# All rows of the second expert table summed by TensorE, with VectorE's share of them removed

## The chip, the cores and the metric

The kernel runs on one core of one Trainium2 chip. The metric is the device time of one execution in microseconds (us), shown as the median of the runs. Engines: PE = TensorE, DVE = VectorE, ACT = ScalarE, POOL = GpSimd, SP = SyncE.

## What is computed

Two transformer blocks on 512 tokens of 1024 features, all in f32. The first has two kinds of attention, cross attention to a memory and a feed-forward part; the second has window attention, gated linear attention and, last, a feed-forward part of looked-up experts (PEER). Only this last part is touched by the change:

```python
q = (h @ wq).reshape(B, S, 8, 2, 128)
sub_scores = einsum('bshpk,hpnk->bshpn', q, subkeys)        # two times 128 keys a head
top_v, top_i = lax.top_k(sub_scores, 16)
cand = top_v[..., 0, :, None] + top_v[..., 1, None, :]      # 16 x 16 sums
best_v, best_pos = lax.top_k(cand, 16)
expert = ...                                                # 16 experts for each of 8 heads: 128 a token
gates = softmax(best_v)
# by blocks of 128 tokens:
ub = take(u, eb)                                            # 128 rows of 1024 for each token
hid = gelu(einsum('tkd,td->tk', ub, xb)) * gb
vb = take(v, eb)
y = einsum('tk,tkd->td', hid, vb)
```

The result is scaled by a row of gates, added to the residual, and normalised.

## The kernel before

The 512 tokens are four blocks of 128, with tokens on the partitions. Everything up to about 1472 us (projections, attentions, feed-forward) is left as it is by the change. The rest is the expert part, one block after another.

**Gather.** POOL (the issue is line 474) fetches, for each block, first the 128 rows of table u and then the 128 rows of table v. One "row" is an indirect DMA that brings each of the 128 tokens its own row of 1024 f32, 512 KB in all. The rows go in turn into a ring of eight slots (RING = 8), so a table is 16 turns (TURNS). Before each issue POOL waits until slot k is free (semaphore slot_free[k]); ahead of each turn it copies eight indices (line 466). The landing raises row_landed[k].

**Up stage.** For each of the 128 rows of u, DVE takes the dot product of row and token (`hidden`, line 1494) and frees the slot. Eight results at a time are copied into `hid`. Then ACT applies gelu (line 737) and DVE multiplies by the gates (`weights`, line 1513), which gives the 128 weights of each token.

**Down stage.** The rows of v are summed with these weights, by two engines that share the slots. SHARED is the list of PE's slots, 1, 3, 5 and 7. For each of these ACT makes a diagonal of 128 weights in `wdiag` (lines 766 to 769; it waits until the slot's row of the turn before has been used) and PE multiplies it with both halves of the row (`add_rows`, line 1095), which adds up in PSUM banks 0 and 1. The rows in slots 0, 2, 4 and 6 are DVE's (`weighted`, line 1523): acc = row * weight + acc, in SBUF. PE takes its rows in order of the slots, DVE its own likewise, and each frees the slot it has used.

**Picking.** `pick(b, q, step)` chooses the experts of one quarter of a block (two heads) in four steps, all on DVE. For block b + 1 its 16 steps are spread over block b's down stage: after each turn of `weighted` comes one step. For block 0 they stand in its up stage. Two additions of the mixer's output for blocks 2 and 3 (`add_mixed`) come after turns 4 and 8 of block 0's down stage.

**End of a block.** `add_experts` (lines 1526 to 1534) waits for slots 7 and 6, adds the two banks to acc (1531), multiplies by the gate row (1533) and adds to the residual X (1534). Behind it on DVE stand the next block's dot products. `prepare` (line 1508) clears acc during each up stage. On PE the late transposes and query projections of blocks 2 and 3 follow block 0's rows and wait for its residual.

```python
for i, k in enumerate(SHARED):
    pe.wait_ge(wdiag_ready, n * len(SHARED) + (len(SHARED) * TURNS * b + i + 1))
    pe.wait_ge(row_landed[k], n * 16 + 16 * (base + 1))
    for half in range(2):
        ins = pe.matmul(bank[half][:], wdiag[:, i, :], ring[k][:, half * COLS:(half + 1) * COLS], ...)
    ins.then_inc(slot_free[k], 1)
```

Of the kernel before, what the change touches and what calls it, by code (L numbers as in the profile page):

```python
# [23 lines left out]
ALU = mybir.AluOpType  # L24
# [41 lines left out]
RING = 8  # L66
TURNS = SLOTS // RING
QUARTERS = 4
CHUNKS = 2 * QUARTERS
SHARED = range(1, RING, 2)  # L70

# [17 lines left out]
def late(*event):  # L91

    return G_OUT2 + LATE.index(event)
# [27 lines left out]
def build(nc, A, out):  # L121
    ctx = ExitStack()
    with ctx:
        def sb(name, shape, dt=F32):
            return ctx.enter_context(nc.sbuf_tensor(name, shape, dt))

        def sem(name):
            return ctx.enter_context(nc.semaphore(name))

        bank = [ctx.enter_context(nc.psum_tensor(f"bank{i}", [P, COLS], F32)) for i in range(8)]  # L130
# [13 lines left out]
        GATE = sb("gate_rows", [P, 2, D])  # L144
# [81 lines left out]
        def scr(lo, n, dt=None, **dims):  # L226
            v = SCR[:, lo:lo + n]
            v = v.bitcast(dt) if dt else v
            return v.rearrange("p (a b) -> p a b", **dims) if dims else v
# [5 lines left out]
        hid, wgt = scr(1184, 128), scr(1312, 128)  # L235
# [4 lines left out]
        ring = [W[:, 2 - 2 * (k // 4), D * (k % 4):D * (k % 4 + 1)] for k in range(RING)]  # L240
        onehot = [t[:, 0:TOPK * CAND].rearrange("p (k c) -> p k c", c=CAND)
                  for t in (levelmask[:].rearrange("p a b -> p (a b)"), SCR[:, 2048:3072])]
        acc = SCR[:, 3072:4096]
        wdiag = GROW[:, 0:P * len(SHARED)].rearrange("p (a b) -> p a b", b=P)

# [7 lines left out]
        row_landed = [sem(f"row_landed{i}") for i in range(RING)]  # L253
# [19 lines left out]
        slot_free = [sem(f"slot_free{i}") for i in range(RING)]  # L273
        hid_copied, hid_ready, hid_gelu, wgt_ready = map(sem, ("hid_copied", "hid_ready", "hid_gelu", "wgt_ready"))
        wdiag_ready = sem("wdiag_ready")
        fin_x, fin_rms, fin_ready = map(sem, ("fin_x", "fin_rms", "fin_ready"))
# [209 lines left out]
        def _(act):  # L486
# [273 lines left out]
            for b in range(NB):  # L760
# [4 lines left out]
                with act.Fori(0, TURNS) as it:  # L765
                    for i, k in enumerate(SHARED):
                        act.wait_ge(slot_free[k], it + (base + 1))
# [14 lines left out]
        def _(pe):  # L782
# [303 lines left out]
            def add_rows(b):  # L1086
# [3 lines left out]
                def turn(n, first, last):  # L1090
# [4 lines that stand above are left out]
                            ins = pe.matmul(bank[half][:], wdiag[:, i, :], ring[k][:, half * COLS:(half + 1) * COLS],  # L1095
                                            start=(first and i == 0), stop=(last and i == len(SHARED) - 1))
                        ins.then_inc(slot_free[k], 1)
# [53 lines left out]
        def _(dve):  # L1151
            steps = [0]

            def link(ins):
                steps[0] += 1
                ins.then_inc(dve_step, 1)
                dve.wait_ge(dve_step, steps[0])
# [102 lines left out]
            for r in range(48):  # L1260
                dve.wait_ge(ada_landed[r % 3], 16 * (r // 3 + 1))
                dve.tensor_tensor_reduce(out=ada[:, r % 3, :], in0=ada[:, r % 3, :], in1=crow, scale=1.0, scalar=0.0,
                                         op0=ALU.mult, op1=ALU.add, accum_out=mod[:, r:r + 1]).then_inc(ada_used, 1)
# [5 lines left out]
            for i, (scale, gc) in enumerate(((8, GC_ATT2), (32, GC_PEER))):  # L1269
                dve.scalar_tensor_tensor(out=scol[:, i, :], in0=mod[:, scale:scale + KT], scalar=1.0, in1=gcol[:, gc, :],  # L1270
                                         op0=ALU.add, op1=ALU.mult)
# [21 lines left out]
            for b in range(NB):  # L1293
                for half in range(2):
                    i = STATS[N_Y] + 2 * b + half
# [3 lines left out]
                    ins = dve.tensor_scalar(y, y, rstd[:, i:i + 1], None, ALU.mult)  # L1299
                ins.then_inc(xn_ready, 1)  # L1300
            for b in range(MB):
                i = STATS[N_MEM] + b
# [37 lines left out]
            for i, gate in enumerate((16, 40)):  # L1340
                for k in range(KT):
                    ins = dve.tensor_scalar(diag[:, i, k * P:(k + 1) * P], ident[:], mod[:, gate + k:gate + k + 1], None, ALU.mult)
# [30 lines left out]
            for n in range(8 * NB):  # L1373
                l, b = n // NB, n % NB
# [11 lines left out]
                for r in range(2):  # L1386
                    half = slice(2 * P * r, 2 * P * (r + 1))
                    ins = dve.tensor_tensor(to[:, half].rearrange("p (h t) -> p h t", h=2),
                                            bank[2 * (n % 4) + r][:, 0:2 * P].rearrange("p (h t) -> p h t", h=2), mask, ALU.mult)
# [3 lines left out]
            for b in range(NB):  # L1393
# [4 lines left out]
                for h in range(GLA_HEADS):  # L1398
                    s = slice(h * GLA_DV, (h + 1) * GLA_DV)
                    ins = dve.scalar_tensor_tensor(out=XN[:, b, COLS + h * GLA_DV:COLS + (h + 1) * GLA_DV], in0=bank[4 + b][:, s],  # L1400
                                                   scalar=rsy[:, b, h:h + 1], in1=gg[:, b, s], op0=ALU.mult, op1=ALU.mult)
                ins.then_inc(go_ready, 1)
            def add_mixed(b):

                dve.wait_ge(proj_out, late("out", b, 1) + 1)
                link(dve.tensor_tensor(XN[:, b, :], XN[:, b, :], GATE[:, 0, :], ALU.mult))
                dve.tensor_tensor(X[:, b, :], X[:, b, :], XN[:, b, :], ALU.add).then_inc(x_ready, 1)
# [80 lines left out]
            def hidden(b, c):  # L1488

                base = TURNS * 2 * b + 2 * c  # L1490
                with dve.Fori(0, 2) as it:
                    for k in range(RING):
                        dve.wait_ge(row_landed[k], it * 16 + 16 * (base + 1))
                        dve.tensor_tensor_reduce(out=ring[k], in0=ring[k], in1=XN[:, b, :], scale=1.0, scalar=0.0,  # L1494
                                                 op0=ALU.mult, op1=ALU.add, accum_out=hslot[:, k:k + 1]).then_inc(slot_free[k], 1)
                    dve.wait_ge(slot_free[RING - 1], it + (base + 2))
                    dve.tensor_copy(hid[:, bass.ds(it * RING + 2 * RING * c, RING)], hslot).then_inc(hid_copied, 1)
                    dve.wait_ge(hid_copied, it + (TURNS * b + 2 * c + 1))

            def prepare(b):  # L1500

                dve.wait_ge(gate_exp, b + 1)
                link(dve.tensor_reduce(gsum, gates, AX.X, ALU.add))
                link(dve.reciprocal(ginv, gsum))
                dve.tensor_tensor(gates, gates, ginv[:, :, None].broadcast_to([P, PEER_HEADS, TOPK]), ALU.mult)
                if b > 0:
                    dve.wait_ge(fin_x, b)
                link(dve.memset(acc, 0.0))

            def weights(b):  # L1510

# [1 line left out]
                dve.tensor_tensor(wgt, hid, gates.rearrange("p h k -> p (h k)"), ALU.mult).then_inc(wgt_ready, 1)  # L1513
                dve.wait_ge(wgt_ready, b + 1)

            def weighted(b, t):

                base = TURNS * (2 * b + 1)
                mine = [k for k in range(RING) if k not in SHARED]
                for i, k in enumerate(mine):  # L1520
                    dve.wait_ge(row_landed[k], t * 16 + 16 * (base + 1))
                    dve.wait_ge(slot_free[mine[i - 1]], t + (base + (2 if i else 1)))
                    dve.scalar_tensor_tensor(out=acc, in0=ring[k], scalar=wgt[:, bass.ds(t * RING + k, 1)],  # L1523
                                             in1=acc, op0=ALU.mult, op1=ALU.add).then_inc(slot_free[k], 1)

            def add_experts(b):
                for k in (RING - 1, RING - 2):
                    dve.wait_ge(slot_free[k], TURNS * 2 * (b + 1) + 1)
                for half in range(2):
                    s = slice(half * COLS, (half + 1) * COLS)  # L1530
                    ins = dve.tensor_tensor(acc[:, s], acc[:, s], bank[half][:], ALU.add)
                link(ins)
                link(dve.tensor_tensor(acc, acc, GATE[:, 1, :], ALU.mult))
                dve.tensor_tensor(X[:, b, :], X[:, b, :], acc, ALU.add).then_inc(fin_x, 1)

            def final_norm(b):
# [11 lines left out]
            for b in range(NB):  # L1548
                dve.wait_ge(proj_out, late("token", b, 1) + 1)
                for c in range(CHUNKS):  # L1550

                    if b == 0:
                        for i in range(4) if c == 0 else range(2 * c + 2, 2 * c + 4):
                            if i < 4 * (QUARTERS - 1):
                                pick(0, i // 4 + 1, i % 4)
                    if c == CHUNKS - 1:
                        prepare(b)
                    hidden(b, c)
                    if b == 1 and c in (1, 2):
                        reciprocal_root(N_PEER, c + 1)  # L1560
                    if b > 0 and c == 0:
                        final_norm(b - 1)
                dve.sem_inc(hid_ready, 1)
                weights(b)
                if b + 1 < NB:

                    for t in range(TURNS):
                        weighted(b, t)
                        pick(b + 1, t // 4, t % 4)
                        if b == 0 and t in (4, 8):  # L1570
                            add_mixed(1 + t // 4)
                else:
                    with dve.Fori(0, TURNS) as it:
                        weighted(b, it)
                add_experts(b)
            final_norm(NB - 1)

# [72 lines left out]
```

## Time and profile before

| | |
|---|---|
| time, median of 3 runs | 3225.07 us (3217.53, 3225.07, 3225.73) |
| span of the profiled execution | 3217.2 us (the page gives no other time of it) |
| busy, share of the span | PE 61%, weight loads 43%, DVE 58%, POOL 49%, ACT 16% |
| mean DMA rate | 207 GB/s over the span; 294 to 337 GB/s in the expert part |
| gathers | 1024 indirect DMAs of 512 KB, 536.94 MB |

The span is the time from the first to the last instruction that the profiler saw. A matmul's end is modelled, so durations of matmuls that overlap add up to more than the time that they take; the distance between their starts is measured. In the rows below, "PEld" are weight loads of PE. "idle ... <- X" is the time for which the engine stood idle before the instruction and what ended most of it. Where an instruction waits for two semaphores, the profile names the one that came last in its own account.

### The profile page before, as it was taken

Reading aid. Unit: us, or ns where it says so; the run is one execution under the profiler, and the core shown is the slowest. Engines: PE = TensorE matmul, PEld = TensorE weight load, DVE = VectorE, ACT = ScalarE, POOL = GpSimd, SP = SyncE. Lnnn points to the kernel's source line nnn. Section 1 sums busy time; section 2 is a strip of 40 time slices with the busy share of each in tenths; the row PEclk is TensorE's granted clock in tenths of the full one; section 3 lists DMA queues with packets and bytes.
Section 4 is the critical chain, followed back from the end, with each engine's and each line's share of the span. In section 5 each row is a group of like instructions: output and inputs, shape, how many; then the busy total and the mean of one; then the engine's idle time right before and its main releaser. Section 6 shows DMA issues by size and latency. Waiting matters only on the chain.

```text
span 3217.2 us, 28826 instructions
## 1 busy us (share of the span) xinstructions
PE 1963.6 (61%) x9164; PEld 1391.7 (43%) x9164; DVE 1855.6 (58%) x3620; ACT 516.6 (16%) x1221; POOL 1573.1 (49%) x1284
## 2 busy tenths in 40 slices
PE   7879989989999899388004650816620066400366
PEld 6756678878989786366001220802210022100122
DVE  5652322245353424818877768776677767777544
ACT  3012333241020324131000110201100011100011
POOL 4220001220000221704777777777777777777775
PEclk9965589999999895599557895869965589755799
DMA  6620013122222130025889998899989899888898
GB/s 228 240 103 1 14 53 123 54 74 94 92 102 84 62 120 19 4 102 172 270 277 329 319 318 304 310 320 323 328 294 315 299 330 333 297 312 312 310 337 298
DMA packets 170786, 665.42 MB, mean 207 GB/s; under 512 B 19616, under 2 KB 20144, under 8 KB 160176
## 3 DMA queue, kind: packets, MB, share of 16 engines
q0 software_dynamic: 147456, 536.94, 47.7%
q1 hardware_dynamic: 23216, 127.00, 10.8%
q8 instruction: 67, 1.10, 0.1%
q14 instruction: 47, 0.39, 0.0%
HBM read 661.76 MB, written 2.10 MB: 206 GB/s over the span
## 4 chain that ended last, share of the span: by engine, by line
PE 37%; POOL 22%; issue 19%; DMA 10%; DVE 9%; ACT 1%; POOLq 1%; SPq 0%; DVEq 0%; ACTq 0%
POOL weights L474 20%; PE bank L808 6%; PE bank L809 6%; PE bank L810 6%; DMA weights<-in_peer_v,scratch 5%; PE bank L899 3%; DMA weights<-in_peer_u,scratch 2%; DVE weights L1494 2%; PE bank L1095 2%; PE bank L882 2%; PE bank L846 1%; PE bank L860 1%; PE bank L866 1%; POOL scratch L466 1%; DMA scratch<-in_w_ada 1%
## 5 line engine op out<-in xcount | busy, mean ns | idle before, releaser
L1095 PE MATMUL bank<-weights,gain_row 128*128 128x512 f32 x1024 | 537.3, 653 | 922.1 <-DMA weights<-in_peer_v,scratch 891.3
L474 POOL DMA_INDIRECT weights<-in_peer_u,scratch x512 | 655.3, 1280 | 221.3 <-issue 148.2
L1095 PEld LDWEIGHTS bank<-weights,gain_row 128*128 128x128 f32 x1024 | 186.6, 202 | 1271.1 <-issue 922.3
L1494 DVE CUSTOM_DVE_ANT_0 weights<-weights,x_norm 128x1024 f32<-128x1024 f32 x512 | 621.8, 1226 | 180.6 <-DMA weights<-in_peer_u,scratch 167.5
L474 POOL DMA_INDIRECT weights<-in_peer_v,scratch x512 | 600.9, 1174 | 192.0 <-issue 122.9
L390 POOL CAST weights_split<-weights 128x2048 fp32r<-128x2048 f32 x25 | 50.8, 2031 | 1000.3 <-DMA weights<-in_w_in 545.3
L1523 DVE SCALAR_TENSOR_TENSOR scratch<-weights,scratch 128x1024 f32<-128x1024 f32 x256 | 329.1, 1286 | 308.0 <-DMA weights<-in_peer_v,scratch 300.8
L808 PE MATMUL bank<-h_T_high,weights_split 128*128 128x512 f32 (+1 forms) x528 | 208.3, 394 | 9.9 <-POOL weights_split L391 7.3
L768 ACT ACTIVATE gain_row<-ident,scratch 128x128 f32<-128x128 f32 x256 | 101.5, 401 | 670.3 <-PE bank L1095 667.8
L809 PE MATMUL bank<-h_T_low,weights_split 128*128 128x512 f32 (+1 forms) x528 | 207.0, 392 | 0.0
L810 PE MATMUL bank<-h_T_high,weights_split 128*128 128x512 f32 (+1 forms) x528 | 206.8, 392 | 0.0
L1177 DVE CAST weights_split<-weights 128x2048 fp32r<-128x2048 f32 x41 | 50.5, 1233 | 209.2 <-DMA weights<-in_w_ff 143.1
L808 PE MATMUL bank<-weights_split,h_T_high 128*128 128x256 f32 x544 | 156.0, 287 | 6.0 <-POOL weights_split L391 2.5
L809 PE MATMUL bank<-weights_split,h_T_high 128*128 128x256 f32 x544 | 155.5, 286 | 0.0
L810 PE MATMUL bank<-weights_split,h_T_low 128*128 128x256 f32 x544 | 155.4, 286 | 0.0
L808 PE MATMUL bank<-weights_split,hidden_high 128*128 128x256 f32 x512 | 146.7, 287 | 5.5 <-DVE hidden_low L1323 5.5
L809 PE MATMUL bank<-weights_split,hidden_high 128*128 128x256 f32 x512 | 146.4, 286 | 0.0
L810 PE MATMUL bank<-weights_split,hidden_low 128*128 128x256 f32 x512 | 146.3, 286 | 0.0
L1133 PE MATMUL bank<-h_T,area 128*128 128x128 f32 x1024 | 121.3, 284 | 34.3 <-issue 34.3
L1133 PEld LDWEIGHTS bank<-h_T,area 128*128 128x128 f32 x1024 | 120.7, 200 | 35.3 <-issue 35.3
L391 POOL TENSOR_TENSOR weights_split<-weights,weights_split 128x2048 fp32r<-128x2048 f32 x25 | 121.4, 4857 | 2.0
L899 PE MATMUL bank<-area,scratch 128*128 128x64 f32 (+1 forms) x496 | 117.4, 393 | 1.2 <-ACT scratch L574 1.1
(259 smaller groups left out, 3382.3 us busy)
## 6 DMA issues: line engine op xcount, KB each, us to landing
weights<-in_w_ff SPq DMA_DIRECT2D x32, 1024.0 KB, 4.8
scratch<-in_w_ada SPq DMA_DIRECT2D x48, 512.0 KB, 5.5
weights<-in_w_in SPq DMA_DIRECT2D x22, 1024.0 KB, 5.4
area<-in_w_pq SPq DMA_DIRECT2D x4, 2048.0 KB, 10.9
weights<-in_peer_u,scratch POOLq DMA_INDIRECT x512, 5.9
weights<-in_peer_v,scratch POOLq DMA_INDIRECT x512, 5.9
weights<-in_w_out SPq DMA_DIRECT2D x4, 1024.0 KB, 6.0
weights<-in_w_mk SPq DMA_DIRECT2D x4, 1024.0 KB, 4.8
```

Of the source, the lines that this page charges most:

```text
L391: pool.tensor_tensor(low, raw, high.bitcast(F32), ALU.subtract).then_inc(w_split, 1)
L474: pool.indirect_dma_start(ring[k], None, src, bass.IndirectOffsetOnAxis(ap=idx[:, turn % 2, k:k + 1], axis=0)).then_inc(row_landed[k], 16)
L768: act.activation(wdiag[:, i, :], ident[:], ACT.Copy, scale=wgt[:, bass.ds(it * RING + k, 1)]).then_inc(wdiag_ready, 1)
L808: pe.matmul(ps, lhs[0], rhs[0], start=start, stop=False)
L809: pe.matmul(ps, lhs[0], rhs[1], start=False, stop=False)
L810: return pe.matmul(ps, lhs[1], rhs[0], start=False, stop=stop)
L882: ins = pe.transpose(bank[3 + u % 2][:, j * P:(j + 1) * P], prob[:, u % 4, j * P:(j + 1) * P], ident[:])
L899: ins = pe.matmul(bank[5 + u % 2][:, 0:v.shape[-1]], probT[:, u % 2, j * P:(j + 1) * P], v, start=(j == 0), stop=(j == n // P - 1))
L1095: ins = pe.matmul(bank[half][:], wdiag[:, i, :], ring[k][:, half * COLS:(half + 1) * COLS], start=(first and i == 0), stop=(last and i == ...
L1133: ins = pe.matmul(ps[:, 0:P], wq[:, i // 4, at:at + P], HT[:, k, b * P:(b + 1) * P], start=(k == 0), stop=(k == KT - 1))
L1494: dve.tensor_tensor_reduce(out=ring[k], in0=ring[k], in1=XN[:, b, :], scale=1.0, scalar=0.0, op0=ALU.mult, op1=ALU.add, accum_out=hslot[:, ...
L1523: dve.scalar_tensor_tensor(out=acc, in0=ring[k], scalar=wgt[:, bass.ds(t * RING + k, 1)], in1=acc, op0=ALU.mult, op1=ALU.add).then_inc(slo ...
```

## The change

PE gets all eight slots, ACT makes eight diagonals a turn instead of four. DVE's `weighted` and the accumulator's clearing are gone; `acc` is now only the place of the product of bank and gate row. DVE runs all 16 steps of picking for the next block one behind the other at the start of the down stage, and ahead of them, in block 0, both `add_mixed`.

```diff
-SHARED = range(1, RING, 2)
+SHARED = range(RING)
...
                 dve.tensor_tensor(gates, gates, ginv[:, :, None].broadcast_to([P, PEER_HEADS, TOPK]), ALU.mult)
-                if b > 0:
-                    dve.wait_ge(fin_x, b)
-                link(dve.memset(acc, 0.0))
...
-            def weighted(b, t):
-
-                base = TURNS * (2 * b + 1)
-                mine = [k for k in range(RING) if k not in SHARED]
-                for i, k in enumerate(mine):
-                    dve.wait_ge(row_landed[k], t * 16 + 16 * (base + 1))
-                    dve.wait_ge(slot_free[mine[i - 1]], t + (base + (2 if i else 1)))
-                    dve.scalar_tensor_tensor(out=acc, in0=ring[k], scalar=wgt[:, bass.ds(t * RING + k, 1)],
-                                             in1=acc, op0=ALU.mult, op1=ALU.add).then_inc(slot_free[k], 1)
...
                 for half in range(2):
                     s = slice(half * COLS, (half + 1) * COLS)
-                    ins = dve.tensor_tensor(acc[:, s], acc[:, s], bank[half][:], ALU.add)
+                    ins = dve.tensor_tensor(acc[:, s], GATE[:, 1, s], bank[half][:], ALU.mult)
                 link(ins)
-                link(dve.tensor_tensor(acc, acc, GATE[:, 1, :], ALU.mult))
                 dve.tensor_tensor(X[:, b, :], X[:, b, :], acc, ALU.add).then_inc(fin_x, 1)
...
                 weights(b)
                 if b + 1 < NB:
 
+                    if b == 0:
+                        add_mixed(2)
+                        add_mixed(3)
                     for t in range(TURNS):
-                        weighted(b, t)
                         pick(b + 1, t // 4, t % 4)
-                        if b == 0 and t in (4, 8):
-                            add_mixed(1 + t // 4)
-                else:
-                    with dve.Fori(0, TURNS) as it:
-                        weighted(b, it)
                 add_experts(b)
```

## Rows read from the trace of the kernel before

**Rows 1.** The page: busy time, share of the span, instructions.

```profile
PE 1963.6 (61%) x9164; PEld 1391.7 (43%) x9164; DVE 1855.6 (58%) x3620; ACT 516.6 (16%) x1221; POOL 1573.1 (49%) x1284
```

**Rows 2.** Busy by stretch, then clock, DMA share, GB/s: down stages, an up stage, projections.

```profile
1723.70:1929.20 205.50, 135.06 (x256) 47.16 (x256) 141.65 (x359) 25.37 (x61) 158.54 (x143) 0.94 0.91 323
2150.60:2354.60 204.00, 131.24 (x259) 46.23 (x260) 136.99 (x355) 25.38 (x61) 156.71 (x144) 0.97 0.92 326
2581.70:2784.30 202.60, 135.34 (x256) 46.59 (x256) 137.21 (x355) 25.37 (x61) 155.60 (x143) 0.94 0.93 329
3009.90:3206.00 196.10, 135.59 (x256) 46.77 (x256) 81.06 (x65) 24.09 (x60) 142.20 (x139) 0.94 0.93 335
2362.60:2578.60 216.00, 0.00 (x0) 0.00 (x0) 162.74 (x278) 4.01 (x5) 167.48 (x139) 0.50 0.87 298
500.00:680.00 180.00, 175.37 (x1008) 155.12 (x1006) 50.81 (x81) 50.09 (x120) 39.67 (x12) 1.00 0.24 86
```

**Rows 3.** Groups of instructions: busy us, mean ns, idle time before and its releasers.

```profile
L474 POOL DMA_INDIRECT weights<-in_peer_u,scratch x512 | 655.3, 1280 | 221.3 <-issue 148.2 <-POOL scratch L466 47.8 <-DVE scratch L1494 24.7
...
L474 POOL DMA_INDIRECT weights<-in_peer_v,scratch x512 | 600.9, 1174 | 192.0 <-issue 122.9 <-POOL scratch L466 51.2 <-PE bank L1095 17.8
L1095 PE MATMUL bank<-weights,gain_row 128*128 128x512 f32 x1024 | 537.3, 653 | 922.1 <-DMA weights<-in_peer_v,scratch 891.3 <-ACT gain_row L768 30.6
L1523 DVE SCALAR_TENSOR_TENSOR scratch<-weights,scratch 128x1024 f32<-128x1024 f32 x256 | 329.1, 1286 | 308.0 <-DMA weights<-in_peer_v,scratch 300.8 <-DVE scratch L1430 2.5 <-issue 1.1
...
L768 ACT ACTIVATE gain_row<-ident,scratch 128x128 f32<-128x128 f32 x256 | 101.5, 401 | 670.3 <-PE bank L1095 667.8 <-DVE scratch L1513 2.5
...
L1533 DVE TENSOR_TENSOR scratch<-scratch,gate_rows 128x1024 f32<-128x1024 f32 x4 | 4.9, 1226 | 0.1
...
L1508 DVE MEMSET scratch<- 128x1024 f32 x4 | 3.6, 912 | 0.7 <-issue 0.7
```

**Rows 4.** Timeline, before the expert part: matmuls of the same shape in a stream.

```profile
1467.69 8.75 PE L846 MATMUL bank<-weights,h_T 128*128 128x512 f32 x20
```

**Rows 5.** Busy by stretch, columns as above: start of the third down stage.

```profile
2581.70:2587.30 5.60, 5.60 (x7) 2.00 (x8) 2.03 (x2) 0.40 (x1) 4.15 (x5) 0.50 0.96 347
```

**Rows 6.** Timeline: starts of three down stages, and first dot products behind two.

```profile
1722.20 1.28 ACT L768 ACTIVATE gain_row<-ident,scratch 128x128 f32<-128x128 f32 x4 [0.62 <-DVE scratch L1513]
...
1723.66 5.39 PE L1095 MATMUL bank<-weights,gain_row 128*128 128x512 f32 x8 [140.48 <-DMA weights<-in_peer_v,scratch]
...
1937.17 1.22 DVE L1494 CUSTOM_DVE_ANT_0 weights<-weights,x_norm 128x1024 f32<-128x1024 f32 x1
...
2147.60 1.28 ACT L768 ACTIVATE gain_row<-ident,scratch 128x128 f32<-128x128 f32 x4 [0.61 <-DVE scratch L1513]
...
2362.54 1.22 DVE L1494 CUSTOM_DVE_ANT_0 weights<-weights,x_norm 128x1024 f32<-128x1024 f32 x1
...
3008.10 1.28 ACT L768 ACTIVATE gain_row<-ident,scratch 128x128 f32<-128x128 f32 x4 [0.61 <-DVE scratch L1513]
```

**Rows 7.** Timeline: start of the third down stage.

```profile
2579.80 1.28 DVE L1523 SCALAR_TENSOR_TENSOR scratch<-weights,scratch 128x1024 f32<-128x1024 f32 x1
2580.06 1.28 ACT L768 ACTIVATE gain_row<-ident,scratch 128x128 f32<-128x128 f32 x4 [0.61 <-DVE scratch L1513]
...
2581.66 8.35 PE L1095 MATMUL bank<-weights,gain_row 128*128 128x512 f32 x12 [223.61 <-DMA weights<-in_peer_v,scratch]
```

**Rows 8.** The tile view of the second table: issue to landing.

```profile
DMA to landing us min/median/max: 4.8/5.9/7.5
```

**Rows 9.** Timeline: end of the third down stage and start of the fourth up stage.

```profile
2782.28 1.95 PE L1095 MATMUL bank<-weights,gain_row 128*128 128x512 f32 x4 [0.53 <-DMA weights<-in_peer_v,scratch]
...
2788.59 1.28 DVE L1531 TENSOR_TENSOR scratch<-scratch,bank 128x512 f32<-128x512 f32 x2
...
2791.16 1.23 DVE L1534 TENSOR_TENSOR x_res<-x_res,scratch 128x1024 f32<-128x1024 f32 x1
2792.31 1.22 DVE L1494 CUSTOM_DVE_ANT_0 weights<-weights,x_norm 128x1024 f32<-128x1024 f32 x1
```

## The prediction

> **What bounds the kernel now.** I began with the busy shares: no engine is above 61%, and that mean covers two different halves of the kernel [rows 1]. The change touches only the expert part, from 1472 us to the end, so I cut that part by stage. An **up stage** (first-table rows, DVE dot products) and a **down stage** (second-table rows, summed) alternate four times. What the reader is to see in the table of stages [rows 2]: in all four down stages the DMA engines are 91 to 93% busy at 323 to 335 GB/s, while PE has 131 to 136 us of 196 to 205. So a down stage is bound by the gather. Its 128 rows take 205.5, 204.0, 202.6 and 196.1 us from PE's first to its last matmul: 1.53 to 1.61 us a row. The groups agree: PE and DVE both idle for rows to land, 891 and 301 us [rows 3]. Where the page names ACT's diagonals as PE's releaser (31 us) I don't believe it: the diagonal then being made is for the slot's next turn.
>
> **Part 1: DVE's 256 multiply-adds go.** 256 x 1.286 us = 329 us of DVE [rows 3]. All of it lies beside the gather, which ends last, so by itself it saves nothing.
>
> **Part 2: PE gets 128 rows a stage instead of 64.** This is the term that decides. A row is two 512-column halves, and the trace has each as two matmul records (1024 records for 256 rows [rows 3]), so four a row. The price of a record is not its 0.59 to 0.65 us, which includes the drain, but the distance between starts. Elsewhere 20 such records, each with a weight load of its own, follow one another in 8.75 us at the full clock [rows 4]: (8.75 - 0.59) / 19 = 0.43 us. A row thus costs PE 4 x 0.429 = 1.716 us. That is **above** the 1.53 to 1.61 us at which rows arrive: with half of them PE had 3.1 us for each 1.7 us of work, with all of them it becomes the bound. 128 x 1.716 = 219.6 us.
> The Trainium skill ("TensorE: Matmul & The Clock Gate", section "Back-to-back issue gap") gives two figures for 512 columns: 216 ns for an isolated matmul, and about 131 ns in a sustained stream of weight load and matmul pairs. Two of the first make 0.43 us a record, as the rows show; by the second a row would cost 4 x 2 x 0.131 = 1.05 us, PE would not be the bound, and the time would be that of the rival "faster" below. The measured stream of 20 is just such a stream, so I go by it.
>
> To the 219.6 come two things. The clock is granted at 0.50 after the long idle time in an up stage [rows 5]; the first eight records take 5.39 us [rows 6] where eight at full clock would take 8 x 0.43 + 0.17 = 3.6, so 1.8 us are lost, and in the third block twelve take 8.35 instead of 5.3, 3.0 lost [rows 7]. I take 2.1. The drain of the last record is 0.17. So first start to last end is **221.9 us**. Behind that I expect the full clock: where PE is busy without a pause it is granted 1.00 over 180 us [rows 2]. PE may start sooner, since it no longer waits for slot 1's row but takes slot 0's, which DVE is using already at 2579.80 while PE starts at 2581.66; the limit is then ACT's first diagonal, 0.40 us after its start [rows 7]. The first matmul falls at about 1722.6, 2148.1, 2580.5 and 3008.7 [rows 6, 7]. Last ends: 1944.5, 2370.0, 2802.4, 3230.6, against 1929.2, 2354.5, 2784.3 and 3206.0 now. **Later by 15.3 + 15.5 + 18.1 + 24.6 = 73.5 us.** The fourth pays most since its gather was fastest.
>
> Will the gather keep up? A slot is free again each 8 x 1.716 = 13.7 us, and its next row must be there seven rows (12.0 us) after PE freed it. From issue to landing are 5.9 us, at most 7.5 [rows 8]; POOL adds its place in line, 1.2 to 2.5 us. That fits with some 2 us to spare, so I cost starvation at nothing; if that cover goes, the cost is up to the clock losses of rival B.
>
> **Part 3: ACT makes 128 diagonals a stage**, 0.40 us each [rows 3], in 1.72 us of PE's time each, one turn ahead: hidden. Only the first lies on the path, as before.
>
> **Part 4: picking moves.** All 16 steps of the next block run at the head of the down stage (and for block 0 both additions of the mixed blocks before them). DVE now has 137 to 142 us of work in a stage with picking and 81 without [rows 2]; so 56 to 61 us of picking, which ends long before 222. The index list is ready much earlier, nobody waits for it. What it frees is the turnover. Now, after PE's last row (2782.28 + 1.95 = 2784.23) DVE still finishes the sixteenth step of picking until 2788.6, then adds the experts (two halves from PSUM, gate, residual), and the first dot product starts at 2792.31: 8.1 us after PE. In the other two turnovers (1929.2 to 1937.17, 2354.5 to 2362.54) it is 8.0 and 8.1 [rows 6, 9]. Afterwards PE's end is followed by the two halves (1.28 us) and the residual (1.23), 2.6 us with the semaphores: **-5.5 x 3 = -16.4 us**. The wait of the addition for slots 7 and 6 now ends with PE alone; behind it on DVE stand the next block's dot products, on these POOL's slots, and on the residual PE's late turns of blocks 2 and 3. The ring is full at that moment in both kernels, so I take the up stage from its first dot product as unchanged (216 us in the third block [rows 2]).
>
> **Part 5: small edits.** The multiplication by the gate is folded into reading PSUM: -1.2 us at the very end, where it lies open [rows 3] (the other three are in part 4). The 0.91 us memset of the accumulator [rows 3] stood in an up stage that waits for rows: nothing. PE's loop body doubles: the branch stays once a turn, hidden behind queued matmuls; bounds 0 to 0.4 us a turn (the rows show no gap near a turn's end in the twelve of [rows 7]), I take 0.
>
> **Sum.** +73.5 - 16.4 - 1.2 = **+56 us**. The profiled execution has a span of 3217.2 us, 7.9 below the median of the runs and 0.3 below the shortest; its own time is not given apart. I add the sum to the median: 3225.1 + 56 = **3281 us**.
>
> **The rivals.**
> A, *faster: PE keeps up.* The point from which it decides is a PE row under 1.53 us. Then each down stage goes at the best gather seen, 196.1 us with DVE nearly silent: -9.4 - 7.9 - 6.5 = -23.8, with -16.4 and -1.2: -41 us, **3184**. For it: POOL issues in 1.17 us on average against 1.28 in up stages [rows 3], and the fourth stage, without picking, is the fastest. Against it: 0.43 us a record, four to a row. Chance 0.03. The Trainium skill ("GPSIMD Engine Reference", section "1. Specifications") says that GpSimd's way to SBUF is shared with DVE instructions of two SBUF inputs, which would explain the faster issue; it speaks for the gather and not for PE.
> B, *slower still: the clock dips.* Today the down stages were granted 0.94 to 0.97 [rows 2], with PE pausing between rows. If PE keeps pausing (rows that land in bursts, picking that slows POOL early on) and gets 0.95, a stage takes 219.6 / 0.95 = 231 instead of 221.9: +37 us, **3318**. Against it: 1.00 over a busy stretch. Chance 0.12.
> C, *each row restarts.* PE now starts a row after a wait, and a first record then takes some 0.08 us more than its pitch. If that stays although the row is there (two semaphores to pass per row), 512 x 0.08 = +41 us: **3322**. Chance 0.10.
> D, *little comes of it:* the turnovers give back more, or starts and rows lie at their cheap bounds so that under 10 us remain. Chance 0.02. A half clock all the way (3.43 us a row, 439 us a stage, some 4150 us) has 0.02.
> The forecast itself has 0.71.
>
> **Range.** Lower end: 2.1 us of clock loss down to 1.7, a turnover nearer 2.3, and the first up rows 3 us sooner each: about 3265. Upper end takes in B and C: 3322. Outside lie A, D and the half clock. A measurement of this kernel can tell about 0.3% (10 us) from no change. Faster by more has A's 0.03, within it 0.03 (D and a mild A), slower the remaining 0.94.
>
> **What would show it.** In the down stages PE should be busy without pause, starts 0.43 us apart and 1.72 a row, waiting for landings almost never; stages near 222 us all alike, the fourth as long as the first; DMA share down to about 0.85 and POOL now waiting for PE's freed slots; granted clock 0.99 behind the first 5 us; 2.6 us from PE's last row to the first dot product; DVE idle for some 150 us of each down stage. I am wrong if PE still idles for landings (B), if starts of rows lie 1.8 apart with all rows landed (C), or if a down stage is under 200 us (A).

## The result, and the profile after

The changed kernel takes 3265.9 us (median of 4 runs, 3262.45 to 3272.45) against 3221.3 us for the kernel before, measured beside it (3197.62 to 3225.73). The ratio is 1.0159 with a 95% interval of 1.0127 to 1.0192: slower by about 51 us. A second measurement (below) gave 3265.2 against 3209.0 us, ratio 1.0182 (1.0146 to 1.0218). The two profiled executions differ by 53.5 us of span, 3270.7 against 3217.2.

The busy shares of the changed kernel, to be held against [rows 1]: PE is up from 61 to 71%, DVE down from 58 to 47%.

```profile
PE 2313.9 (71%) x10188; PEld 1597.7 (49%) x10188; DVE 1522.2 (47%) x3356; ACT 617.9 (19%) x1477; POOL 1455.3 (44%) x1284
```

The stages of the changed kernel, cut from PE's first to its last matmul as in [rows 2] (busy us and count of PE, weight loads, DVE, ACT, POOL; then granted clock, DMA share, GB/s): four down stages, then the up stages of the third and the second block.

```profile
1718.10:1940.10 222.00, 221.82 (x512) 97.95 (x512) 65.45 (x302) 51.61 (x129) 129.80 (x146) 0.99 0.88 308
2164.60:2386.90 222.30, 222.30 (x515) 98.54 (x516) 60.69 (x294) 51.44 (x128) 130.41 (x146) 0.99 0.87 308
2602.30:2824.20 221.90, 221.72 (x512) 97.91 (x512) 60.58 (x294) 51.59 (x129) 131.07 (x147) 0.99 0.87 309
3038.50:3260.70 222.20, 222.08 (x512) 97.97 (x512) 0.03 (x1) 49.98 (x127) 118.55 (x139) 0.99 0.84 297
2389.40:2600.30 210.90, 0.91 (x9) 0.71 (x7) 161.91 (x277) 3.96 (x5) 161.67 (x139) 0.51 0.89 307
1942.60:2162.40 219.80, 69.45 (x576) 68.66 (x576) 161.98 (x278) 25.63 (x65) 172.36 (x139) 0.65 0.87 296
```

What is to be seen: the down stages, which took 205.5, 204.0, 202.6 and 196.1 us with PE two thirds busy, take 222 us each, all alike, and PE is busy for the whole of it. The DMA share, which lay between 0.91 and 0.93, now lies between 0.84 and 0.88: the gather waits now. The timeline on PE merges a whole stage into one line, 512 records without a pause:

```profile
1718.01 221.91 PE L1095 MATMUL bank<-weights,gain_row 128*128 128x512 f32 x512 [137.91 <-ACT gain_row L768]
...
3038.37 222.21 PE L1095 MATMUL bank<-weights,gain_row 128*128 128x512 f32 x512 [214.35 <-ACT gain_row L768]
```

The groups of instructions that answer to [rows 3] (busy us, mean ns, idle time before and what ended it):

```profile
L1095 PE MATMUL bank<-weights,gain_row 128*128 128x512 f32 x2048 | 888.2, 597 | 633.9 <-ACT gain_row L768 633.9
L474 POOL DMA_INDIRECT weights<-in_peer_u,scratch x512 | 646.2, 1262 | 224.0 <-issue 143.7 <-POOL scratch L466 47.7 <-DVE scratch L1494 18.5
...
L474 POOL DMA_INDIRECT weights<-in_peer_v,scratch x512 | 498.4, 973 | 358.7 <-PE bank L1095 237.7 <-issue 71.4 <-POOL scratch L466 49.6
...
L768 ACT ACTIVATE gain_row<-ident,scratch 128x128 f32<-128x128 f32 x512 | 202.5, 401 | 637.6 <-PE bank L1095 635.1 <-DVE scratch L1510 2.5
```

The 633.9 us that stand at ACT are only the idle time ahead of the four first matmuls of a stage, mostly an up stage (137.91 and 214.35 us in the lines above), which ends with the first diagonal. The same holds for most of the 891 us at landings before: of PE's 922 us of idle time 651 lay ahead of the four first matmuls (140.48 and 223.61 us in [rows 6] and [rows 7]), and 271 us inside the stages. These 271 us are gone: inside a stage PE now has no idle time at all. POOL on the other hand now waits 238 us for slots that PE frees (18 before); that is the other side of the same thing. And an issue for the second table takes 0.97 us instead of 1.17, which I come back to. A row lands 5.4 us after its issue instead of 5.9 [rows 8]:

```profile
DMA to landing us min/median/max: 4.2/5.4/6.8
```

The start of the third down stage, answering to [rows 7], and its end with the first dot product behind it, answering to [rows 9]:

```profile
2601.66 2.44 ACT L768 ACTIVATE gain_row<-ident,scratch 128x128 f32<-128x128 f32 x8 [0.61 <-DVE scratch L1510]
...
2602.16 4.28 PE L1095 MATMUL bank<-weights,gain_row 128*128 128x512 f32 x5 [211.85 <-ACT gain_row L768]
...
2821.71 2.31 PE L1095 MATMUL bank<-weights,gain_row 128*128 128x512 f32 x5
...
2824.06 1.28 DVE L1518 TENSOR_TENSOR scratch<-gate_rows,bank 128x512 f32<-128x512 f32 x2 [159.26 <-PE bank L1095]
...
2825.38 1.22 DVE L1520 TENSOR_TENSOR x_res<-x_res,scratch 128x1024 f32<-128x1024 f32 x1
...
2826.52 1.22 DVE L1494 CUSTOM_DVE_ANT_0 weights<-weights,x_norm 128x1024 f32<-128x1024 f32 x1
```

PE starts 0.5 us after ACT begins its first diagonal (1.6 before), and the first dot product starts 2.5 us after PE's last end, instead of 8.1; DVE had been idle for 159 us.

The 53.5 us by parts, in differences of the two traces (the differences are taken before rounding):

| part | before | after | difference |
|---|---|---|---|
| four down stages | 205.5, 203.9, 202.6, 196.1 | 221.9, 222.2, 221.9, 222.2 | +80.2 |
| end of the last dot product to first matmul | 3.0, 4.5, 3.1, 3.3 | 2.0, 2.2, 2.1, 2.0 | -5.6 |
| three turnovers | 8.0, 8.1, 8.1 | 2.5, 2.5, 2.5 | -16.6 |
| end behind the last row | 11.3 | 10.1 | -1.2 |
| four up stages | 234.2, 208.9, 216.0, 214.3 | 231.0, 219.9, 210.9, 209.8 | -1.8 |
| all before the first dot product | 1486.5 | 1485.0 | -1.5 |

### The profile page after: what moved, and what is told of

Its sections match the earlier page's. It is cut to its first block, busy times and chain, and to the rows that moved or that the text cites. A ratio compares the mean times of both kernels' runs of the same rounds, so it can differ in the third digit from the quotient of the medians.

```text
span 3270.7 us, 31234 instructions
## 1 busy us (share of the span) xinstructions
PE 2313.9 (71%) x10188; PEld 1597.7 (49%) x10188; DVE 1522.2 (47%) x3356; ACT 617.9 (19%) x1477; POOL 1455.3 (44%) x1284
## 3 DMA queue, kind: packets, MB, share of 16 engines
q8 instruction: 69, 1.13, 0.1%
## 4 chain that ended last, share of the span: by engine, by line
PE 61%; POOL 13%; issue 11%; DVE 8%; DMA 5%; ACT 1%; POOLq 0%; SPq 0%; DVEq 0%; ACTq 0%
PE bank L1095 27%; POOL weights L474 10%; PE bank L808 6%; PE bank L809 6%; PE bank L810 6%; PE bank L899 3%; DMA weights<-in_peer_u,scratch 2%; DVE weights L1494 2%; PE bank L882 2%; PE bank L846 1%; PE bank L860 1%; PE bank L866 1%; DMA scratch<-in_w_ada 1%; DVE scratch L1262 1%; PE bank L872 1%
## 5 line engine op out<-in xcount | busy, mean ns | idle before, releaser
L1095 PE MATMUL bank<-weights,gain_row 128*128 128x512 f32 x2048 | 888.2, 597 | 633.9 <-ACT gain_row L768 633.9
L1095 PEld LDWEIGHTS bank<-weights,gain_row 128*128 128x128 f32 x2048 | 392.4, 192 | 1127.9 <-issue 1127.9
L474 POOL DMA_INDIRECT weights<-in_peer_u,scratch x512 | 646.2, 1262 | 224.0 <-issue 143.7
L474 POOL DMA_INDIRECT weights<-in_peer_v,scratch x512 | 498.4, 973 | 358.7 <-PE bank L1095 237.7
L768 ACT ACTIVATE gain_row<-ident,scratch 128x128 f32<-128x128 f32 x512 | 202.5, 401 | 637.6 <-PE bank L1095 635.1
## 6 DMA issues: line engine op xcount, KB each, us to landing
area<-in_w_pq SPq DMA_DIRECT2D x4, 2048.0 KB, 11.4
```

The costliest lines, as they stand in the source:

```text
L474: pool.indirect_dma_start(ring[k], None, src, bass.IndirectOffsetOnAxis(ap=idx[:, turn % 2, k:k + 1], axis=0)).then_inc(row_landed[k], 16)
L768: act.activation(wdiag[:, i, :], ident[:], ACT.Copy, scale=wgt[:, bass.ds(it * RING + k, 1)]).then_inc(wdiag_ready, 1)
```

## The experiments

All were timed beside the kernel before. My theory (P) was that PE's own work per row sets the down stage. Its rivals: the handshakes of each row do, that is, PE's waits for semaphores before a row (H), or the change made the gather slower (G). In the first experiments (up to the form with one record) the kernel before had a median of 3220.8 us; the others ran on another chip, where it had 3209.0 us. Ratios are each to the kernel before on the same chip.

**Half of each row.** The changed kernel, with one edit:

```diff
-                        for half in range(2):
+                        for half in range(1):
```

> The changed kernel, with PE multiplying only the first 512 columns of each row (the second half of the expert sum is left out, and what DVE reads from the second bank is old). Two records a row instead of four, 0.86 us instead of 1.716; diagonals, waits, picking and DVE's part are the same. Theory P (PE's own work per row sets the down stage): PE drops below the gather's 1.53 to 1.61 us a row, the four down stages fall from 222 to the gather's pace, 190 to 200 us, and the kernel ends some 26 us x 4 = 105 us sooner than the changed one: about 3165 us, ratio to before 0.983. Rival H (the handshake sets it: each row waits for its diagonal and its two semaphores): down stages stay at 215 to 222, ratio to before 1.012 to 1.016. Rival G (picking in one piece disturbs POOL's issues, and the gather became slower): down stages stay over 210 as well.

3138.1 us, ratio 0.9767 (0.9726 to 0.9808). The four down stages take 186.8, 187.9, 189.0 and 185.9 us. Two of them (same columns as above) and the issues for the second table:

```profile
1723.50:1910.30 186.80, 144.85 (x256) 41.08 (x256) 65.57 (x302) 50.32 (x129) 126.38 (x143) 0.96 0.96 356
2934.20:3120.10 185.90, 147.75 (x256) 43.50 (x256) 0.02 (x1) 48.02 (x127) 118.57 (x138) 0.93 0.94 354
```

```profile
L474 POOL DMA_INDIRECT weights<-in_peer_v,scratch x512 | 499.5, 976 | 243.7 <-issue 167.9 <-remote 55.9 <-POOL scratch L466 16.8
```

With the same diagonals and the same two waits a row, the stage falls from 222 to between 186 and 189 us. H and G are out. But P expected 190 to 200 us and about 3165 in all: the gather is faster than in any stage of the kernel before, 354 to 356 GB/s in the two stages shown against 323 to 335. That was new, and the later runs go after it.

**Picking one turn sooner, in the kernel before.**

```diff
                     for t in range(TURNS):
                         weighted(b, t)
-                        pick(b + 1, t // 4, t % 4)
+                        for s in (0, 1) if t == 0 else (t + 1,) if t + 1 < TURNS else ():
+                            pick(b + 1, s // 4, s % 4)
```

> The kernel before, sharing as it was, with picking one turn sooner: steps 0 and 1 behind turn 0, step t+1 behind turn t. Nothing is removed. Only the turnover between a down stage and the next up stage should change: now 8.1 us from PE's last row to the first dot product, of which 4.3 are the last step of picking. Theory P with its part 4: turnover 3.8 us, three times -4.3 = -13 us, ratio 0.996, down stages as before (196 to 205). Rival T (the turnover is no loss: the first rows of the up stage are gathered meanwhile, and the up stage gets longer by what the turnover gets shorter): ratio 1.000, up stages 4 us longer.

3211.8 us, ratio 0.9976 (0.9953 to 1.0000). The turnover behind the third down stage, which ends here at 2782.48 + 1.96:

```profile
2782.48 1.96 PE L1095 MATMUL bank<-weights,gain_row 128*128 128x512 f32 x4 [0.91 <-DMA weights<-in_peer_v,scratch]
...
2784.47 1.28 DVE L1531 TENSOR_TENSOR scratch<-scratch,bank 128x512 f32<-128x512 f32 x2 [2.04 <-PE bank L1095]
...
2788.19 1.22 DVE L1494 CUSTOM_DVE_ANT_0 weights<-weights,x_norm 128x1024 f32<-128x1024 f32 x1
```

3.8 us instead of 8.1, as it should be. The down stages took 205.2, 203.6, 210.4 and 192.3 us: the third is longer and the fourth shorter than the 196 to 205 that I expected. The time can't separate 0.996 from 1.000, and this profile doesn't rule out rival T either: its turnovers are 12.9 us shorter and its four up stages 7.2 us longer (880.6 us against 873.4). Over all nine profiles with a short turnover the four up stages add up to 849 to 881 us, mostly less than in the kernel before, so they don't grow as a rule; but they scatter by more than the turnover gives back. That the turnover's gain reaches the total in full is not shown.

**Six slots for PE, two for DVE** (with picking sooner).

```diff
-SHARED = range(1, RING, 2)
+SHARED = [k for k in range(RING) if k not in (2, 6)]
```

> As the kernel with picking sooner, and PE has six slots of eight (0, 1, 3, 4, 5, 7), DVE two (2, 6). PE needs 6 x 1.716 = 10.3 us a turn, under the gather's 12.3. Theory P: PE is not the bound, the down stages are the gather's, and because DVE has 128 multiply-adds less beside POOL's issues they go to 195 to 200 us: with -13 of the turnover about -25 to -30 us, ratio 0.991. Rival D (DVE's load doesn't matter to the gather): as the kernel with picking sooner, 0.996. Rival H (per-row handshakes cost PE more than its records): over 1.000, stages beyond 205 us.

3173.1 us, ratio 0.9858 (0.9825 to 0.9890), better than both kernels and than P's own figure of 0.991. Its four down stages:

```profile
1725.10:1922.20 197.10, 175.16 (x384) 69.72 (x384) 106.51 (x334) 38.72 (x97) 144.78 (x144) 0.99 0.94 341
2144.40:2347.30 202.90, 177.82 (x387) 71.67 (x388) 101.81 (x330) 38.66 (x96) 147.91 (x145) 0.97 0.93 333
2559.00:2755.60 196.60, 179.43 (x384) 71.61 (x384) 101.66 (x330) 38.56 (x96) 143.26 (x145) 0.97 0.94 342
2977.50:3168.90 191.40, 173.98 (x384) 70.04 (x384) 41.41 (x33) 36.91 (x95) 132.30 (x138) 0.99 0.93 345
```

PE still has pauses (175 of 197 us), and the gather runs at 333 to 345 GB/s. Two stages lie outside P's 195 to 200 us, 202.9 above and 191.4 below. Against the run before, which also picks sooner, the four down stages are 23 us shorter in all (788 against 811): sharing six to two helps the gather. That speaks against rival D, but it settles D only if the gain comes from DVE's 128 multiply-adds less and not from PE freeing more of the slots. This run changes both; the last run of this section tests the load alone.

**One record a half row.** The changed kernel; `ringr` and `GROWR` are views of the same memory in fp32r, a second way of reading f32 data, which PE takes here in one record instead of two. The lines of the last two pairs are shortened.

```diff
+        ringr = [WS[:, 2 - 2 * (k // 4), D * (k % 4):D * (k % 4 + 1)] for k in range(RING)]
-        wdiag = GROW[:, 0:P * len(SHARED)].rearrange("p (a b) -> p a b", b=P)
+        wdiag = GROWR[:, 0:P * len(SHARED)].rearrange("p (a b) -> p a b", b=P)
...
-pool.indirect_dma_start(ring[k], None, src, ...)
+pool.indirect_dma_start(ringr[k] if table else ring[k], None, src.bitcast(F32R) if table else src, ...)
...
-ins = pe.matmul(bank[half][:], wdiag[:, i, :], ring[k][:, half * COLS:(half + 1) * COLS], ...)
+ins = pe.matmul(bank[half][:], wdiag[:, i, :], ringr[k][:, half * COLS:(half + 1) * COLS], ...)
```

> The changed kernel, but diagonal and row are read by PE as fp32r, the form that this kernel's projections use, where a 128x512 matmul of 0.39 us is one record and starts lie 0.23 us apart (so the sums are made of operands of reduced precision). Everything else, all columns and all waits, is the changed kernel's. A row then costs PE 2 x 0.23 = 0.46 us. Theory P: down stages at the gather's pace, 190 to 200 us each, about 3165 us, ratio 0.983, as with half the columns: below a row's 1.5 us it no longer matters how little PE has. Rivals H and G: down stages stay over 210 us and the ratio over 1.005.

3137.0 us, ratio 0.9760 (0.9721 to 0.9799), the same as with half of the columns left out, and once more below P's 0.983. All four down stages, and the issues for the second table:

```profile
1719.60:1908.40 188.80, 152.46 (x256) 63.86 (x256) 65.39 (x301) 49.02 (x128) 127.38 (x143) 0.50 1.05 355
2123.00:2312.30 189.30, 152.48 (x259) 64.64 (x260) 61.25 (x293) 49.25 (x128) 129.41 (x144) 0.50 1.05 352
2529.30:2718.00 188.70, 152.35 (x256) 63.83 (x256) 61.10 (x293) 49.76 (x128) 129.40 (x145) 0.50 1.05 356
2930.80:3113.90 183.10, 151.31 (x256) 63.83 (x256) 0.15 (x1) 48.81 (x126) 118.91 (x138) 0.51 1.05 358
```

```profile
L476 POOL DMA_INDIRECT weights_split<-in_peer_v,scratch x512 | 502.3, 981 | 238.0 <-issue 167.8 <-remote 52.3 <-POOL scratch L468 14.8
```

This is the change with everything that it does, except for the price of a row on PE. Where PE isn't the bound, the change is worth 2.4%. The clock is at 0.50 nearly throughout (256 records in 189 us, with pauses between). A row is therefore not as cheap as I had expected: PE is busy for 152 us of a stage, 1.19 us a row instead of 0.46. It costs nothing, since a row arrives every 1.43 to 1.48 us; with half of the columns, at a granted clock of 0.93 to 0.96, the stages were no shorter (186 to 189 us).

**The changed kernel again.** No edit.

> The changed kernel once more, unaltered, for the spread of what the change doesn't touch. Theory P: down stages 222 us each again to within 0.5 us, turnovers 2.5, since PE's own work sets them; all scatter lies in the up stages (206 to 235 us in the profiles so far). Ratio 1.012 to 1.018. If the 11 us that the second block's up stage was longer than before came from the change, they are there again (about 220 us); if from scatter, it lies elsewhere between 206 and 220.

3265.2 us, ratio 1.0182 (1.0146 to 1.0218). First and last down stage, and the second block's up stage:

```profile
1717.90:1939.90 222.00, 221.94 (x512) 97.89 (x512) 65.44 (x302) 51.65 (x129) 129.37 (x146) 0.99 0.87 309
...
3016.80:3239.60 222.80, 222.72 (x512) 98.19 (x512) 0.00 (x0) 50.05 (x127) 118.54 (x138) 0.99 0.83 295
1942.40:2148.20 205.80, 67.26 (x576) 66.47 (x576) 161.85 (x279) 25.73 (x65) 158.00 (x141) 0.67 0.90 317
```

Down stages 222.0 to 222.9 (I had written within 0.5; it is 0.9) and the second block's up stage 205.8 us instead of 219.8. So the 11 us longer up stage of the first profile was scatter and not the change: an issue of the first table took 1.30 us there on average and 1.19 here. This span, 3249.6 us, is 21 us below that of the first profile, since the four up stages add up to 22.9 us less (the down stages to 1.9 more).

**Six records a row.**

```diff
                             ins = pe.matmul(bank[half][:], wdiag[:, i, :], ring[k][...], ...)
+                            if half == 0:
+                                pe.matmul(bank[2][:], wdiag[:, i, :], ring[k][:, 0:COLS], start=True, stop=True)
```

> The changed kernel with the first half of every row multiplied a second time, into a spare bank that nobody reads: six records a row instead of four. Theory P: 6 x 0.429 = 2.57 us a row, 128 rows 329.5, with the slow start 331.5 us a down stage, +110 us each, the kernel about 3705 us (+440). Rival H (handshakes have a part in the 222): less than 110 us more a stage.

3698.9 us (one run; P's figure was 3705). Its first down stage; the others are 332.8, 331.9 and 332.3 us:

```profile
1721.40:2052.90 331.50, 331.38 (x768) 146.29 (x768) 65.46 (x302) 51.59 (x129) 128.97 (x146) 1.00 0.70 209
```

+109.5 us for 256 records more: 0.428 us each (all four stages: +440.3 us for 1024, 0.430). At this price the 512 records of the changed kernel are 219 to 220 of their 222 us, and the slow start is the rest. The traces say the same directly: behind the first records of a stage, starts lie 0.429 us apart within a row and from row to row alike, in all four stages of the changed kernel. Nothing is left for handshakes.

**Seven slots for PE, one for DVE** (with picking sooner).

```diff
-SHARED = range(1, RING, 2)
+SHARED = [k for k in range(RING) if k not in (6,)]
```

> As the run with six slots, with seven for PE and slot 6 alone for DVE: PE has 7 x 1.716 = 12.0 us a turn, 16 turns 192.2 and 194.5 with the slow start. The gather alone did 187 us beside a silent DVE and 191 to 203 with two slots on DVE. Theory P: PE and the gather are level here, stages 195 to 202 us, ratio 0.985 to 0.99, no better than six. Rival (only the number of rows that DVE has counts, through POOL's issues): clearly faster than six, stages 190 us, ratio 0.975 to 0.98.

3166.8 us, ratio 0.9870 (0.9839 to 0.9902), not to be told from six, as P had it. Its first and last down stages, and the last on PE's timeline:

```profile
1722.90:1917.50 194.60, 194.44 (x448) 85.67 (x448) 86.19 (x318) 45.27 (x113) 136.18 (x146) 0.99 0.95 350
...
2956.90:3152.30 195.40, 195.21 (x448) 86.03 (x448) 20.71 (x17) 43.68 (x111) 122.46 (x137) 0.99 0.92 335
```

```profile
2956.73 195.38 PE L1095 MATMUL bank<-weights,gain_row 128*128 128x512 f32 x448 [216.79 <-ACT gain_row L768]
```

The four stages are 194.6, 194.3, 195.7 and 195.4 us, and PE is without a pause once more (0.3 us in the third stage): 448 x 0.429 = 192.2, and 2.1 to 3.5 for the slow start and the pause. The bound changes hands between six and seven rows of eight.

**DVE beside the gather.** The kernel with one record a half row, and on DVE, behind picking:

```diff
+            def beside(b):
+                base = TURNS * (2 * b + 1)
...
+                with dve.Fori(0, TURNS) as it:
+                    for k in range(0, RING, 2):
+                        dve.wait_ge(row_landed[k], it * 16 + 16 * (base + 1))
+                        ins = dve.scalar_tensor_tensor(out=acc, in0=XN[:, b, :], scalar=wgt[:, bass.ds(it * RING + k, 1)],
+                                                       in1=acc, op0=ALU.mult, op1=ALU.add)
...
+                beside(b)
                 add_experts(b)
```

> The kernel with one record a half row, and DVE beside it makes four multiply-adds of 1024 columns a turn, of tokens instead of rows, into the accumulator, each when a row has landed; nobody waits for them and the accumulator is overwritten afterwards. Slots, PE and ACT as without them. Theory Q (the silence of DVE makes the gather faster: down stages 183 to 189 us at 0.95 to 0.99 us an issue, against 196 to 205 at 1.12 to 1.21 before): in the fourth block, where there is no picking, the stage goes from 183 to 192 to 197 us and an issue from 0.95 to about 1.1; over the four blocks +25 to +45 us, ratio 0.985 to 0.99. Rival R (the gather gets faster because PE frees the slots sooner or in order, not because of DVE): unchanged, 183 to 189 us, ratio 0.976.

3159.0 us, ratio 0.9843 (0.9793 to 0.9892). Stages and issues:

```profile
1718.10:1913.60 195.50, 152.77 (x256) 64.07 (x256) 149.12 (x366) 51.60 (x129) 148.23 (x144) 0.50 1.03 343
2123.90:2321.20 197.30, 151.85 (x257) 64.28 (x258) 144.07 (x359) 51.50 (x129) 150.01 (x144) 0.51 1.02 338
2534.70:2731.00 196.30, 152.84 (x256) 64.12 (x256) 144.15 (x359) 51.62 (x129) 148.92 (x144) 0.50 1.03 340
2948.40:3142.00 193.60, 152.48 (x256) 64.25 (x256) 82.98 (x65) 49.96 (x127) 139.72 (x139) 0.50 1.02 340
```

```profile
L477 POOL DMA_INDIRECT weights_split<-in_peer_v,scratch x512 | 570.7, 1115 | 191.0 <-issue 129.9 <-POOL scratch L469 51.9 <-PE bank L1098 9.1
```

Nobody waits for these multiply-adds, and yet the four stages are 6.7, 8.0, 7.6 and 10.5 us longer than in the run without them (33 us in all), and an issue takes 1.12 us instead of 0.98. The fourth stage, without picking, shows it within one profile: the 105 issues that overlap in time with a multiply-add took 1.13 us on average, the 23 others 0.97. The two runs were on different chips, but that can't be the cause: on the chip of the slower one the kernel before was the faster by 12 us. So the load on DVE, by itself, slows the gather, and rival R as the only cause is out. It isn't out as a part: from the kernel before (808 us for its four down stages) to one record without the load (750) are 58 us, and the load explains 33. The other 25 may come from the order and the time at which slots are freed, or from picking in one piece; no run here separates these.

## Why the prediction was right

The forecast was +56 us. The ratio of the first measurement says about 51, its medians 44.6; the second measurement says 58 and 56.3. The runs of the kernel before scatter over 28 us in the first measurement alone, so the total confirms the size only roughly. That the two profiled spans differ by 53.5 us is in part luck. The second profile of the same changed kernel is 21 us shorter, by its up stages, and against it the difference would have been 32. What confirms the prediction is the sum part by part, in the stages that hardly scatter.

The time of 3281 us is 15 above the median of 3265.9. Of these 3.8 lie in the start of the sum (3225.1 against 3221.3 us for the kernel before) and 11.4 in the difference; the medians can't say more of it, though the scatter of the up stages is large enough. The lower end of the range was also set lower than its own terms give: 4 x 0.4, 3 x 0.3 and 3 us for each of three or four up stages are 11.5 to 14.5 us, which leads to 3267 to 3270 and not to 3265. Both medians, 3265.9 and 3265.2 us, lie just below that. That the range holds them is luck.

- **Part 2, the term that decides**, held: 221.9 us were forecast from the pitch of 20 unrelated matmuls and a slow start, 221.9 to 222.2 were measured in the first profile and 222.0 to 222.9 in the second. What varies is the slow start alone, 2.1 in the forecast, 2.0 to 3.0 in these eight stages. Six records (331.5) and seven slots (194.6) fit the same line. The figure of 216 ns for 512 columns of "TensorE: Matmul & The Clock Gate" (the Trainium skill, section "Back-to-back issue gap"), two of them a record, agrees; its 131 ns for a sustained stream does not appear here.
- **The earlier starts** were put at 5.8 us in all (inside the +73.5), and were 5.6. (By the rows that are named, two of them, 2148.1 and 3008.7, should have been 2148.0 and 3008.5; it changes nothing.)
- **Keeping up**: starvation at nothing was right; no pause in the 512 records of any stage.
- **Part 4**: turnovers 2.6 us forecast, 2.5 measured; -16.4 against -16.6. **Part 5**: -1.2, as forecast; the longer loop body costs nothing (no gap in the merged line). The reason that was given for this had no ground: twelve records are three rows, and a turn of the kernel before has four of PE's rows, so those twelve don't reach a turn's end.
- **Rivals B and C** did not come: granted clock 0.99 over the stage, and rows follow one another without the 0.08 us.
- **Read too large** were PE's 891 us of waits for landings: 271 us of idle time lay inside the down stages (a third of their 808 us), the rest in the up stages. That the stages were not PE's follows from the 271 us just as well.
- **Wrong was the reasoning of part 1**, that DVE's 329 us "by itself saves nothing" because it lies beside the gather. Here it did save nothing, but only since PE had become the bound. The gather's own pace went from 196 to 205 us a stage before to 183 to 189 where DVE sums no rows and PE keeps up, 58 us in all, and the runs with one record a half row, without and with DVE's load, put 33 us of that on the load. So rival A's price, 3184 us, taken from the fastest stage seen, was too high: where PE keeps up the time is 3137 us.

So the change holds a gain of 77 to 84 us (by the ratio and by the medians, 3221 to 3137) and a new bound that takes it back and 45 to 58 us more. Six slots on PE, with picking one turn sooner and all operands in f32 as before, takes 1.4% off the kernel before; the form with one record takes 2.4%, but it reads the operands as fp32r, and what that does to the precision of the sums is not measured here.

## What to carry to other kernels

Before work is moved to another engine, compare that engine's distance between starts, times the count, with the pace at which its input arrives; its share of busy time over the whole kernel (61% here) says nothing of it. A split of the work is tuned to where the two meet: 4 of 8 rows left DVE in the gather's way, 8 of 8 made PE the bound, and 6 and 7 were the best of the splits tried in f32 (5 was not tried). An engine that is off the path may still slow the one on it: measure that by adding its load back where nobody waits for it.

## What was not expected of the hardware

DVE's multiply-adds slow POOL's issues of indirect DMAs. An issue took 0.98 us where DVE only picked (0.95 in the fourth stage, where it had nothing to do), 1.12 us with 64 multiply-adds a stage (f32, two inputs in SBUF) beside that (1.10 in the fourth stage), and 1.17 us in the kernel before. "GPSIMD Engine Reference" (the Trainium skill, section "1. Specifications") says that GpSimd shares its way to SBUF with DVE instructions of two SBUF inputs; these runs agree, though they don't show by which way the slowdown comes. That the gather is bound by the issues alone isn't shown either: in the fastest stage it moved 358 GB/s.
